# Attention with the keys on partitions, row maxima from a second set of queries-first scores in two passes

## The reference, cut to what matters

```python
def one_block(qblk):
    s = jnp.einsum('bkgqd,bskd->bkgqs', qblk, k).astype(jnp.float32) * scale
    p = jax.nn.softmax(s, axis=-1).astype(v.dtype)
    return jnp.einsum('bkgqs,bskd->bkgqd', p, v)
```

## Time and profile before

| what | value |
|---|---|
| median of 3 executions | 3549.56 us (3543.59 to 3550.28) |
| the profiled execution | 3547.59 us |
| its span, first to last instruction | 3545.8 us |
| PE, PEld busy over the span | 89%, 82% |
| DVE, ACT, POOL busy over the span | 53%, 47%, 11% |

### The profile page before, as it was taken

How to read it: one execution, slowest core, us unless ns; L and a number is a source line. 1 busy time by engine, 2 the same in 40 slices (tenths; PEclk the granted TensorE clock), 3 DMA queues, 4 the chain that set the end, 5 groups by cost and what they waited for, 6 DMA issues and landing times. The chain is left out here.

```text
span 3545.8 us, 60756 instructions
## 1 busy us (share of the span) xinstructions
PE 3171.3 (89%) x21856; PEld 2900.2 (82%) x21856; DVE 1878.6 (53%) x3485; ACT 1671.7 (47%) x3239; POOL 388.6 (11%) x400
## 2 busy tenths in 40 slices
PE   6999994759999999999699756999999999999991
PEld 6788883748888888888588645999999999999991
DVE  2222226548888888888533365545455445545443
ACT  2222220547777777777434202455455544455442
POOL 0333333500000000000000000010010000110001
PEclk9999997869999999999799855999999999999996
DMA  5121113410000000000244204565565555665545
GB/s 217 43 80 60 67 66 116 140 42 25 27 27 27 27 27 27 27 27 27 81 147 150 83 0 132 174 192 185 179 198 184 183 187 179 188 193 181 181 130 220
DMA packets 307599, 393.69 MB, mean 111 GB/s; under 512 B 13808, under 2 KB 263872, under 8 KB 306496
## 3 DMA queue, kind: packets, MB, share of 16 engines
q1 hardware_dynamic: 293680, 338.64, 28.9%
q0 software_dynamic: 10240, 35.66, 4.4%
q10 hardware_dynamic: 3600, 18.35, 1.3%
HBM read 318.68 MB, written 74.06 MB: 111 GB/s over the span
## 5 line engine op out<-in xcount | busy, mean ns | idle before, releaser
L2304 DVE TENSOR_TENSOR e_w_lo<-e_raw,e_w_hi 128x2048 fp32r<-128x2048 f32 x192 | 440.1, 2292 | 490.4 <-ACT e_w_hi L2246 490.4
L92 PE MATMUL e_ps<-e_x_hi,e_w_hi 128*128 128x272 f32 x2048 | 602.1, 294 | 5.5 <-issue 5.5
L94 PE MATMUL e_ps<-e_x_hi,e_w_lo 128*128 128x272 f32 x2048 | 593.8, 290 | 0.0
L93 PE MATMUL e_ps<-e_x_lo,e_w_hi 128*128 128x272 f32 x2048 | 590.1, 288 | 0.0
L2246 ACT ACTIVATE e_w_hi<-e_raw 128x2048 fp32r<-128x2048 f32 x192 | 366.1, 1907 | 163.7 <-DMA e_raw<-in_w_gate 159.3
L1470 DVE TENSOR_TENSOR a_pT_lo<-a_ps_t,a_pT_hi 128x512 fp32r<-128x512 f32 (+1 forms) x648 | 368.0, 601 | 139.5 <-ACT a_pT_hi L1368 139.2
L1368 ACT ACTIVATE a_pT_hi<-a_ps_t 128x512 fp32r<-128x512 f32 (+1 forms) x648 | 319.6, 532 | 185.1 <-PE a_ps_t L1238 180.5
L92 PEld LDWEIGHTS e_ps<-e_x_hi,e_w_hi 128*128 128x128 f32 x2048 | 386.1, 189 | 7.1 <-issue 5.5
L93 PEld LDWEIGHTS e_ps<-e_x_lo,e_w_hi 128*128 128x128 f32 x2048 | 386.9, 189 | 0.0
L94 PEld LDWEIGHTS e_ps<-e_x_hi,e_w_lo 128*128 128x128 f32 x2048 | 385.8, 188 | 0.0
L1443 DVE TENSOR_REDUCE a_mx<-a_ps_s 128x1 f32<-128x896 f32 (+2 forms) x392 | 346.1, 890 | 26.8 <-PE a_ps_s L1228 26.8
(11 more groups left out here) (269 smaller groups left out, 5478.2 us busy)
## 6 DMA issues: line engine op xcount, KB each, us to landing
e_raw<-in_w_gate SPq DMA_DIRECT2D x64, 1024.0 KB, 5.2
e_raw<-in_w_up SPq DMA_DIRECT2D x64, 1024.0 KB, 5.2
e_raw<-in_w_down SPq DMA_DIRECT2D x64, 1024.0 KB, 5.2
a_wm<-in_w_mod SPq DMA_DIRECT2D x32, 512.0 KB, 4.0
s_ret<-p_pr SPq DMA_DIRECT2D x17, 768.0 KB, 3.6
m_raw<-in_w_in ACTq DMA_DIRECT2D x8, 1152.0 KB, 7.1
o_cT<-s_ct SPq DMA_DIRECT2D x17, 512.0 KB, 4.7
s_x<-o_x SPq DMA_DIRECT2D x17, 512.0 KB, 4.9
```

Of the source, the lines that this page charges most:

```text
L92: nc.tensor.matmul(out, w_hi, x_hi, start=first, stop=False)
L93: nc.tensor.matmul(out, w_hi, x_lo, start=False, stop=False)
L94: return nc.tensor.matmul(out, w_lo, x_hi, start=False, stop=last)
L2304: nc.vector.tensor_tensor(w_lo[n % RING][:, :, :], raw[n % RING][:, :, :], w_hi[n % RING][:, :, :].bitcast(F32), ALU.subtract).then_inc(w_ ...
```

## The change

The stage is rewritten so that the scores used for the probabilities come out with keys on partitions, which is already the layout the product with the values wants. A row maximum cannot be taken across partitions, so the queries-first scores are formed as well, only to take the maxima. The unit is now a slot: one tile of 128 queries and one key/value head v, thus 4 query heads or `QCOLS` = 512 columns; a tile has 2 slots, and there are 32 latent slots. In a slot:

- `rough(i, v, n)`: 20 pieces, one matmul pair each, of the queries-first scores of the *next* slot (L1210, L1212), into two single banks `ps_r`. DVE takes each piece's maximum (`maxima`, L1497), then the maximum of the five pieces of each head (`tops`, L1507).
- `turn_top`: PE transposes the maxima into a row (L1220); ACT writes it, negated, as row 64 of `qM` (`keep_top`, L1382). `keys_lo` has ones in row 64.
- `scores`: for each of 17 key tiles two matmuls of 512 columns (L1233, L1234); the second one's row of ones times the row of maxima subtracts the maximum. Two key tiles make a pair; a slot has 9 pairs (the last one has one tile), in two double banks `ps_s`.
- ACT takes exp of a pair at once, 128x1024, into a ring of three (`exps`, L1395), and copies it rounded to `p_hi` (`high`, L1407), now from SBUF. DVE forms `p_lo` = prob - p_hi (`low`, L1514), now with both inputs in SBUF.
- `value`: 17 tiles x 2 parts, each 512 columns (L1250), two pairs behind the scores.
- Row sums: GpSimd adds the pairs up, element by element (`add`, L1148: 7 additions of 128x1024 and 2 of 128x512 a slot), and 4 float32 matmuls with a column of ones finish them (L1265). `combine` takes the reciprocal from PSUM.
- All small products (queries, modulation, fold, out, top) share one bank `ps_m` and one pair of semaphores.
- Preparation: ACT rounds the keys of a tile before it copies the tile before it (`round_keys`, `keep_keys`), so that two tiles are under way.

```diff
-            def scores(i, h, seg, q_uses):
-                        ins = nc.tensor.matmul(ps_s[:, b, 0:w], qT[:, h, :], keys[:, part, h // QPK, src:src + w],
-                                               start=(part == 0), stop=(part == 1))
-            def turn(i, h, n, bank):
-                    ins = nc.tensor.transpose(ps_t[b][:, c % 4, :], prob[h % 2][:, c * P:(c + 1) * P], g["ident"][:, :])
+            def rough(i, v, n):
+                if not (first_slot(i, v) and n < 2):
+                    pe.wait_ge(max_ok, piece(i, v, n) - 1)
+                nc.tensor.matmul(ps_r[n % 2][:, 0:w], qT[v][:, h * P:(h + 1) * P], keys[:, v, src:src + w],
+                                 start=True, stop=False)
+                nc.tensor.matmul(ps_r[n % 2][:, 0:w], qM[v][0:HD, h * P:(h + 1) * P], keys_lo[0:HD, v, src:src + w],
+                                 start=False, stop=True).then_inc(rough_ok, 1)
+            def scores(i, v, j, t):
+                if t == 0 and not (first_slot(i, v) and j < 2):
+                    pe.wait_ge(exped, n - 1)
+                nc.tensor.matmul(ps_s[b][:, t, :], keys[:, v, src * P:(src + 1) * P], qT[v][:, :], start=True, stop=False)
+                ins = nc.tensor.matmul(ps_s[b][:, t, :], keys_lo[:, v, src * P:(src + 1) * P], qM[v][:, :],
+                                       start=False, stop=True)
...
+                    if j == PAIRS - 1:
+                        turn_top(*ahead)
...
+                    if j == 2:
+                        modulation(i, v)
+                    if j == 3 and not first_slot(i, v):
+                        fold_halves(*last)
...
+            def add(i, v, r, out, x, y):
+                n = pair(i, v, 0) + r
+                if r:
+                    pool.wait_ge(folded, n)
+                nc.gpsimd.tensor_tensor(out, x, y, ALU.add).then_inc(folded, 1)
...
-                    nc.vector.tensor_tensor(pT_lo[h // 2 % 2][:, out, h % 2, :], ps_t[b][:, 0:m, :],
-                                            pT_hi[h // 2 % 2][:, out, h % 2, :].bitcast(F32), ALU.subtract)\
+                nc.vector.tensor_tensor(p_lo[:, at, 0:m, :], prob[:, at % RING, 0:m, :], p_hi[:, at, 0:m, :].bitcast(F32),
+                                        ALU.subtract).then_inc(lo_ok, 1)
```

More of the change, by code:

```diff
@@ L1108, in mod_use, with first_slot, ctx_tile, quad @@
-        def mod_use(i, n):
-            bank = Bank(i)
-            return {e: use for h in range(NQ) for e, use in bank.step(i, h).items()}["mod", n]
-        def group_index(i, n):
-            return i * NGRP + n
-        def tiles(eng, body):
+        def first_slot(i, v):
+            return isinstance(i, int) and i == 0 and v == 0
+        def ctx_tile(i):
+            return isinstance(i, int) and i == NT
+        def quad(i, v):
+            return 2 * i + v
+        def before(i, v):
+            return (i, 0) if v else (i - 1, 1)
@@ L1144, in body @@
[L1144 to L1165 removed]
+                    sp.wait_ge(q_lo_ok, i)
@@ new lines, in fold_halves @@
+            def fold_halves(i, v):
+                pe.wait_ge(o_kept, quad(i, v) + 1)
+                if not ctx_tile(i):
+                    pe.wait_ge(folded, pair(i, v, 0) + PAIRS)
+                pe.wait_ge(emptied, use_of_fold(i, v))
+                for c in range(QPK):
+                    nc.tensor.matmul(ps_m[:, c * HD:(c + 1) * HD], o_sum[:, c * P:(c + 1) * P], fold[:, :], start=True, stop=True)
+                for c in range(QPK):
+                    rows = prob[:, v, 0, c * P:(c + 1) * P] if ctx_tile(i) else acc_all[:, c * P:(c + 1) * P]
+                    ins = nc.tensor.matmul(ps_m[:, QPK * HD + c:QPK * HD + c + 1], rows, ones[:, :], start=True, stop=True)
+                ins.then_inc(filled, 1)
@@ new lines, in body @@
+            def body(i):
+                for v in range(NKV):
+                    slot(i, v)
+            slots(pe, body)
+            for t in range(2):
+                value(NT - 1, 1, PAIRS - 2, t)
+            turn_queries(NT, 1)
+            scores(NT, 0, 0, 0)
+            value(NT - 1, 1, PAIRS - 1, 0)
+            for n in range(QPK):
+                rough(NT, 1, n)
+            fold_halves(NT - 1, 1)
+            value(NT, 0, 0, 0)
+            turn_out(NT - 1, 1)
+            turn_top(NT, 1)
@@ L1531, in _ @@
+            def body(i):
+                for v in range(NKV):
+                    slot(i, v)
+            slots(dve, body)
+            low(NT - 1, 1, PAIRS - 1)
+            copy_queries(NT, 1)
+            low(NT, 0, 0)
+            for n in range(QPK):
+                maxima(NT, 1, n)
+            tops(NT, 1)
+            combine(NT - 1, 1)
+            low(NT, 1, 0)
+            combine(NT, 0)
+            combine(NT, 1)
             second_gain()
```

713 lines of the change are left out of this document (355 added, 358 removed).

## The result

| | median | lowest to highest |
|---|---|---|
| before, 4 executions | 3548.57 us | 3543.59 to 3550.28 |
| after, 4 executions | 4309.23 us | 4307.88 to 4326.19 |
| after / before | 1.2157 | 95%: 1.2124 to 1.2190 |

The changed kernel is 761 us slower. The forecast was 3595 us with a range of 3530 to 3650, so the direction was right and the size was not near. The span of the profiled execution is 4306.1 us.

A forecast was written before the change was run, and what follows sets the result against it. It took PE's list to bound the kernel: 28.4 us a slot plus 3.3 of waiting is 31.7, so 32 slots add 67 us; outside the loop saves 19.5; net +47.7 gives 3595 us, range 3530 to 3650.

The forecast's parts named there:

- TensorE's list: PE's work in the loop: 28.4 us a slot, 56.8 a tile, against 53.0 before.
- rough 17,408 columns, 7.94: Rough scores of a slot on TensorE: 4 heads x 2176 x 2 columns, priced at 7.94 us.
- took the upper level for granted: TensorE's clock in the loop: matmuls priced at the upper of two levels, granted 1.00, 0.2335 us for 512 columns.
- matmuls of 512 columns further apart than 0.2335: TensorE in the loop: a sign that the forecast is wrong, spacing above or below 0.2335 us.
- the 3.3 us of waiting in the sum: Waiting per slot: steps 1, 4, 5 and 6 plus 1.7 us at the seam, 3.3 us together.
- The exclusion: GpSimd additions and DVE remainders block each other when both read two SBUF operands: 27.9 us a slot of shared path.
- the price of an addition: GpSimd's row sums in a slot: 2.44 us for an addition of 1024 columns.
- the third rival: Seam of a slot: remainder 6 comes behind addition 7, another 2.3 us; 34.0 a slot, 3669 us; chance 0.15.
- The first (no cost of the exclusion): Loop: exclusion falls into VectorE's waits, only 1.2 us waiting; 29.6 a slot, 3528 us; chance 0.17.
- Outside the loop: Preparation and ends, first rounding to last store without the slots: 69.8 us against 89.3 before, -19.5.
- the key tiles at 1.82 us for 1.8: Preparation, two key tiles under way: 1.8 us each instead of 2.88, 32.4 us for 18.

The follow-up runs named there:

- e1: The changed kernel with 65 instead of 64 rows in the second rough matmul and one more copy a slot: 3819.3 us, 1.0765 of before.
- e2: The kernel before with 64 rows instead of 128 in the second pass of its scores: 3808.4 us, 1.0738 of before.
- e8: The changed kernel, 64 rows kept, without GpSimd's additions (row sums constant): 4228.5 us, 1.1929 of before.
- e4: e1 without GpSimd's additions (row sums constant): 3574.3 us, 1.0076 of before.
- e5: e1 with the exponential written back in PSUM, so the remainder has one SBUF input, and GpSimd adding up p_hi: 3607.9 us, 1.0169 of before.
- e6: e5 without the second pass of the rough scores: 3521.6 us, 0.9922 of before.
- e9: e2 with 65 rows instead of 64 in the second pass of the scores: 3573.9 us, 1.0073 of before.

## Why the prediction was wrong

**TensorE's list.** Its count of columns and their price hold: 0.23 us for 512 columns at the upper level, 0.64 for the triple of e1. The step that failed is "rough 17,408 columns, 7.94": it priced the 64-row matmul by its columns like all others, though the diff shows `qM[v][0:HD]`, 64 rows. It costs 0.39 us more each at the upper level, 7.8 us a slot. The trace of before had signs of it, in other stages. TensorE's weight loads in order of time, in the retention and in the experts, of before:

```profile
623.35 0.71 PEld L896 LDWEIGHTS r_ps_b<-ident,r_qfb 128*128 128x128 f32 x4 [18.48 <-issue]
...
624.40 0.94 PEld L907 LDWEIGHTS r_ps_s<-r_qkT 64*128 64x128 f32 x8 [0.33 <-issue]
...
2182.36 0.50 PEld L2174 LDWEIGHTS e_ps_t<-ident,e_xg 16*128 16x128 f32 x3 [0.33 <-issue]
```

Where loads of 64 rows, or of 16, follow ones of 128, the first one stands idle for 0.33 us with nothing to wait for; inside the run of eight there is no such gap. But the granted clock is 0.50 in both places. Loads of L907 again, behind others of 128 rows, where it is 1.00:

```profile
642.16 0.30 PEld L931 LDWEIGHTS r_ps_kv<-r_state,r_qfbT 128*128 128x128 f32 x2
642.58 0.53 PEld L907 LDWEIGHTS r_ps_s<-r_qkT 64*128 64x128 f32 x8
```

The first line ends at 642.46, so the gap is 0.12 us, and it is 0.12 again before the next load of 128 rows (643.23). The matmuls have only 128 columns. A search of before for tiles of fewer than 128 rows would have found these rows, and two gaps of 0.12 for each of 20 pieces, 4.8 us a slot, could have stood in the sum as a first estimate. What a change costs between matmuls of 448 and 512 columns, these rows don't show; e2 measured it afterwards.

**The clock.** The prediction took the upper level for granted since before stood at 1.00. The list of things that would make it wrong named matmuls of 512 columns further apart than 0.2335; they are, at 0.427, in two thirds of the slot. This is the largest part: of the 22.0 us that are missing, e8 gives 14.5 to the clock and 7.8 to the exposed loads, while the additions cost 3.0 in place of the 3.3 us of waiting in the sum (31.7 + 14.5 + 7.8 - 0.3 = 53.7). Both came in the main from one cause, the 64 rows, as e1, e8 and e4 show; neither was a rival. That the wait term nearly meets what the additions cost in after is luck: with 65 rows they cost 7.6.

**The exclusion.** Its mechanism, read from an instruction of 1 us, holds for these shapes, and the price of an addition was right (2.37 us for 2.44). Its effect on the slot was mis-sized: stalls of 3.3 us were summed, with 65 rows they and what follows come to 38.3 - 28.4 = 9.9, of which 2.3 remain without additions. The error has two parts: at the seam the race is lost as the third rival had it, and the waiting pulls the clock down, which no case contained. The Trainium skill's rule ("SBUF — State Buffer", section "Who interferes with whom") is borne out by e5: with one input in PSUM the block is gone.

**The rivals.** The first (no cost of the exclusion) can be checked by e4: 30.7 us a slot, where 29.6 was worked out, and 3574 us, still slower than before. The third rival's 34.0 was the nearest to e1's 38.3, which holds the clock as well.

**Outside the loop.** 73 us for 69.8; the key tiles at 1.82 us for 1.8. Right.

So without the 64 rows the change would cost 7.7% and not 1.3. With the exclusion taken away too it would cost 1.7% (e5), and 0.8% with no additions at all (e4); TensorE's list is 56.8 us a tile against 53.0. That part of the reasoning stands: as built, the change gives TensorE nothing back. Of the versions tried, only the one that takes the row maxima from one pass as well pays (e6).

## What to carry to other kernels

Look at the row counts of neighbouring matmuls, not only at their columns: where a 64-row one stands between others, pad it by a row of zeros or group equal ones, and compare PEld's busy share and its "issue" idle time. When the cost of a stall on TensorE is worked out, add what the granted clock does afterwards, since the stalls of e1 doubled in price that way. When GpSimd and VectorE both stream from SBUF, leave one of VectorE's operands in PSUM rather than ordering the two by semaphores.

## What the runs showed of the hardware that was not expected

- A matmul of 64 rows between ones of 128 or 65 has its weights loaded only 0.30 us after the start of the matmul before, and the next one's weights come 0.40 us after its own start, where 448 columns take 0.20: 0.34 (e2) to 0.39 us (after) per change there and back at the upper clock level, 0.60 at the lower. With 65 rows no such gap is seen, but e9's clock fell to 0.96 all the same.
- With 20 such changes in 36 us of work the granted clock stood at 0.67 although the matmul records left 1.2 of 600 us free (e8).
- The exclusion between GpSimd and VectorE holds for whole instructions of 2.4 and 1.2 us: single remainders of 3.41 us, additions of 512 columns at 2.07 to 2.09 instead of 1.28, and a copy of 64x512 with a single input at 1.41 instead of 0.42.
